# Two-model kernel on one core: a mixer's token-major weight chunks reshaped to 512 outputs, and three stretches of hand-written engine order rewritten

## The chip, the core and the metric

The kernel runs on one core of one Trainium2 chip. The time is the device time of one execution in microseconds; lower is better. The core has a matrix engine (TensorE, called PE in the rows), a vector engine (VectorE, DVE), an activation engine (ScalarE, ACT), a general engine (GpSimd, POOL) and a queue engine (SyncE, SP). DMAs are issued from SP, ACT and POOL.

## What is computed

Two stacked blocks over x of 256 tokens by 1024 features. The first block is one layer of sliding-window attention with sinks and a gated FFN; the second has a two-headed mixer ("ab"), an FFN with squared ReLU, latent attention ("c"), and a second such FFN. In the reference, cut to the part around the change:

```python
def ab_mixer(h, w_in, conv_w, gate_b, head_g, v_g, ws, bs, w_out):
    p = h @ w_in                                   # 1024 -> 3088
    qk, va, oa, gates, uv = jnp.split(p, [2*A_WIDTH, 3*A_WIDTH, 4*A_WIDTH, 4*A_WIDTH + 4*A_HEADS], axis=-1)
    qk = jax.nn.silu(centred_dwconv(qk, conv_w))   # five taps along the tokens
    g = (gates + gate_b)                           # 16 columns: input and forget gates, both ways
    ...
    h_fwd = mlstm_scan(q, k, v, li_f, lf_f)        # and backwards
    ha = rms_norm_2(h_fwd + h_bwd, head_g) * jax.nn.sigmoid(oa)
    u, vb = jnp.split(jax.nn.gelu(uv), 2, axis=-1)
    vb = rms_norm_2(vb, v_g)
    sp = jnp.einsum("gts,bnsgc->bntgc", ws, vb) + bs.T[:, :, None]
    hb = u * sp
    return jnp.concatenate([ha, hb], axis=-1) @ w_out
```

## The kernel before

All weights stream through four slots of 2048 columns each (`SLOTS`, `SLOT`). A chunk of weights is 1 MB: it is loaded by SP into `w_raw`, ACT copies it to `w_hi` in the reduced format that TensorE multiplies (`high`, L682), DVE forms the rest `w_lo = w_raw - w_hi` (`low`, L1209, a "low" in what follows), and TensorE makes three products, hi by hi, lo by hi, hi by lo (`product`, L1921 to L1923). SP may refill a slot when its low is done, ACT may overwrite `w_hi` when the matmuls of the slot's last chunk are done. The two token tiles (128 tokens each) are called t = 0 and 1.

Each engine runs its list in the order in which the code is written; `wait_ge` on a semaphore holds back everything behind it on that engine. `high_upto(n)` and `low_upto(n)` put the conversions of all chunks up to n at that place of the list. So the order in the source is the schedule.

Three stretches matter.

The end of the attention: `out_part(i, t, j)` multiplies chunk i of the output weights for token tile t and half j of the 1024 outputs into bank 4 + 2t + j. When a tile's two halves are complete, DVE adds them to the residual, ACT squares, POOL forms `mean_sq` and `rstd` (L555, L556), DVE normalises (L1229), and TensorE transposes the tile (L1992). `enter` on PE, ACT and DVE carries this into the FFN's first two chunks.

The mixer's input: thirteen chunks `c[0]` to `c[12]`. `c[0]`, `c[1]` (values v) and `c[2]`, `c[3]` (values vb) are token-major: the tokens are the stationary operand and 256 weight columns move (`plain_visit`). `c[4]` is the 16 gate columns, `c[5]` to `c[8]` are q and k, `c[9]`, `c[10]` are u, `c[11]`, `c[12]` the output gate, all feature-major (`projection`). After `c[4]` ACT adds the gate bias (`g_raw`, L935) and sends the rows by four small DMAs to `g4` (L938). DVE then takes minus the absolute value of the forget gates (L1566), ACT the exponential and logarithm (L944, L945), and DVE the running sums and maxima (`gate_rows`, L1573 to L1584). `conv(i)` (L1556) is the convolution of `c[5 + i]`. TensorE needs `g_rows_ready` after `c[8]`. The rest of the mixer follows: `decay_rows` (L2304), `scores_T`, `summed` (L2332), `spatial_mixing` (L2343, needs `vn_ready`, DVE L1617), `outputs_T` (L2373, needs `hn_ready`, DVE L1666).

The mixer's output: `operand_out(o[k], ...)` over four chunks in the order 2, 3, 0, 1 of the operand, whose low parts are `full_low` (L1612), counted by `ab_lo`.

Of the kernel before, what the change touches and what calls it, by code (L numbers as in the profile page):

```python
# [19 lines left out]
F32 = mybir.dt.float32  # L20
# [49 lines left out]
def weight_schedule():  # L70
# [65 lines left out]
def build(nc, t_in, out):  # L136
# [3 lines left out]
    with ctx:  # L140
# [287 lines left out]
        def _(sp):  # L428
# [51 lines left out]
            with sp.Fori(0, N1 - 3) as it:  # L480
# [10 lines left out]
            at = ([i * CW for i in (4, 5)] + [uv + i * CW for i in (2, 3)] + [4 * AW] + [i * CW for i in range(4)]  # L491
                  + [uv + i * CW for i in (0, 1)] + [3 * AW, 3 * AW + CW])
            for a, ch in zip(at, sched["ab_in"]):
                load(ch, cols(w, a, ch.shape[1]))
# [44 lines left out]
        def _(pool):  # L539
# [81 lines left out]

            def masks(h):
# [24 lines left out]
            next_gain(5)  # L647
# [5 lines left out]
            for i, (t, j) in enumerate(LATENTS):  # L653
                pool.wait_ge(S["c_ssq"], i + 1)
                step(pool.tensor_scalar(c_ms[:, t, j:j + 1], c_ss[:, t, j:j + 1], c_ev[:, t:t + 1], 0.0, ALU.add, ALU.add))
                pool.tensor_tensor(c_rs[:, t, j:j + 1], c_ms[:, t, j:j + 1], minus_half[:, 0:1], ALU.pow).then_inc(S["c_rstd"], 1)
            for n in range(QUADS):
# [8 lines left out]
        def _(act):  # L666
# [57 lines left out]
            def enter(use, n, early, then):  # L724

                sum_squares(n, 0)
                transposed_high(use, 0, (0,))
                sum_squares(n, 1, (0,))
                transposed_high(use, 0, (1,))
                sum_squares(n, 1, (1,))  # L730
                high_upto(early)
# [102 lines left out]
            enter(1, 1, 0, c[3].index + 1)  # L834
# [55 lines left out]
            def mixing_values(i):  # L890
                ch = c[i]
                act.wait_ge(S["mm_done"], ch.index + 1)
                for t in range(NT):
                    last = act.activation(ab_v1[:, t, 2 * i:2 * i + 2, 0:AD],
                                          bank[AB_BANK[i]][:, t * 256:t * 256 + 256].rearrange("p (a b) -> p a b", a=2),
                                          ACT.Copy, scale=ab_rc[:, t:t + 1])
                last.then_inc(S["v1_ready"], 1)

            def spatial_values(i):
                ch = c[2 + i]  # L900
                act.wait_ge(S["mm_done"], ch.index + 1)
                for t in range(NT):
                    last = act.activation(ab_vb[:, t, i * CW:(i + 1) * CW], bank[AB_BANK[2 + i]][:, t * CW:(t + 1) * CW],
                                          ACT.Gelu_apprx_tanh, scale=ab_rc[:, t:t + 1])
                last.then_inc(S["vb_ready"], 1)
# [1746 lines left out]
```

## Time and profile before

| | |
|---|---|
| median of three runs | 880.72 us (879.99 to 880.95) |
| the profiled execution | 878.9 us |
| its span, first to last instruction | 877.2 us |
| PE busy | 858.1 us |
| mean granted TensorE clock over the span | 0.994 of full |

The profiled execution is 1.8 us faster than the median, and 1.7 us of its time lie outside the span. A busy PE means that some matmul is in flight; matmuls overlap, so the pace is read from the distance between starts, not from the length of one. An engine's idle time is put down to what ended it. Times in rows are counted from the span's start.

### The profile page before, as it was taken

Reading aid. Unit: us, or ns where it says so; the run is one execution under the profiler, and the core shown is the slowest. Engines: PE = TensorE matmul, PEld = TensorE weight load, DVE = VectorE, ACT = ScalarE, POOL = GpSimd, SP = SyncE. Lnnn points to the kernel's source line nnn. Section 1 sums busy time; section 2 is a strip of 40 time slices with the busy share of each in tenths; the row PEclk is TensorE's granted clock in tenths of the full one; section 3 lists DMA queues with packets and bytes.
Section 4 is the critical chain, followed back from the end, with each engine's and each line's share of the span. In section 5 each row is a group of like instructions: output and inputs, shape, how many; then the busy total and the mean of one; then the engine's idle time right before and its main releaser. Section 6 shows DMA issues by size and latency. Waiting matters only on the chain.

```text
span 877.2 us, 14208 instructions
## 1 busy us (share of the span) xinstructions
PE 858.1 (98%) x5784; PEld 774.5 (88%) x5784; DVE 541.6 (62%) x590; ACT 434.5 (50%) x595; POOL 48.1 (5%) x113
## 2 busy tenths in 40 slices
PE   8999999999999989999999999999999999999996
PEld 8977899999998988889999999999867999999995
DVE  5897554444448669777765555567576675555553
ACT  6675443343344785553744444436465364444431
POOL 2200000000001100310000000003000000000000
PEclk9999999999999998999999999999999999999999
DMA  9644355545555655337575555453602576555601
GB/s 314 226 155 147 121 182 190 193 156 191 188 192 148 221 164 174 115 98 216 177 247 183 184 187 189 135 169 105 230 1 91 195 229 195 181 184 183 190 38 49
DMA packets 98442, 147.68 MB, mean 168 GB/s; under 512 B 4042, under 2 KB 81938, under 8 KB 98402
## 3 DMA queue, kind: packets, MB, share of 16 engines
q1 hardware_dynamic: 97234, 143.11, 50.0%
q0 software_dynamic: 1120, 4.00, 1.6%
q8 instruction: 28, 0.46, 0.2%
q14 instruction: 12, 0.10, 0.0%
q10 hardware_dynamic: 48, 0.02, 0.0%
HBM read 146.05 MB, written 1.05 MB: 168 GB/s over the span
## 4 chain that ended last, share of the span: by engine, by line
PE 92%; DVE 4%; ACT 1%; POOL 1%; issue 1%; DMA 1%; ACTq 0%; DVEq 0%; POOLq 0%
PE bank L1921 28%; PE bank L1922 27%; PE bank L1923 27%; PE bank L1992 1%; PE bank L2579 1%; PE bank L2602 1%; PE bank L2564 1%; PE bank L2558 1%; PE bank L2121 1%; PE bank L2140 1%; DMA x_norm<-arena 1%; DVE w_lo L1209 1%; PE bank L2332 0%; PE bank L2304 0%; PE bank L2044 0%
## 5 line engine op out<-in xcount | busy, mean ns | idle before, releaser
L1209 DVE TENSOR_TENSOR w_lo<-w_raw,w_hi 128x2048 fp32r<-128x2048 f32 (+3 forms) x129 | 289.5, 2252 | 150.9 <-ACT w_hi L682 150.7
L1921 PE MATMUL bank<-xT_hi,w_hi 128*128 128x256 f32 x1068 | 306.0, 286 | 4.3 <-DVE w_lo L1209 4.2
L1923 PE MATMUL bank<-xT_hi,w_lo 128*128 128x256 f32 x1068 | 304.0, 285 | 0.0
L1922 PE MATMUL bank<-xT_lo,w_hi 128*128 128x256 f32 x1068 | 304.0, 285 | 0.0
L682 ACT ACTIVATE w_hi<-w_raw 128x2048 fp32r<-128x2048 f32 (+3 forms) x129 | 241.2, 1877 | 92.4 <-PE bank L1923 85.2
L1921 PEld LDWEIGHTS bank<-xT_hi,w_hi 128*128 128x128 f32 x1068 | 205.6, 192 | 9.3 <-DVE w_lo L1209 4.4
L1922 PEld LDWEIGHTS bank<-xT_lo,w_hi 128*128 128x128 f32 x1068 | 205.7, 193 | 1.9 <-issue 0.2
L1923 PEld LDWEIGHTS bank<-xT_hi,w_lo 128*128 128x128 f32 x1068 | 205.6, 193 | 0.2
L1921 PE MATMUL bank<-w_hi,ff_hi 128*128 128x512 f32 x344 | 134.8, 392 | 0.0
L1922 PE MATMUL bank<-w_lo,ff_hi 128*128 128x512 f32 x344 | 134.5, 391 | 0.0
L1923 PE MATMUL bank<-w_hi,ff_lo 128*128 128x512 f32 x344 | 134.0, 390 | 0.0
L1921 PE MATMUL bank<-w_hi,xT_hi 128*128 128x512 f32 (+3 forms) x216 | 76.0, 352 | 2.3 <-DVE w_lo L1332 1.5
L1923 PEld LDWEIGHTS bank<-w_hi,ff_lo 128*128 128x128 f32 x344 | 64.7, 188 | 13.8
L1921 PEld LDWEIGHTS bank<-w_hi,ff_hi 128*128 128x128 f32 x344 | 64.8, 188 | 12.6 <-issue 0.3
L1922 PEld LDWEIGHTS bank<-w_lo,ff_hi 128*128 128x128 f32 x344 | 64.8, 188 | 11.7
L1923 PE MATMUL bank<-w_hi,xT_lo 128*128 128x512 f32 (+3 forms) x216 | 73.4, 340 | 0.0
L1922 PE MATMUL bank<-w_lo,xT_hi 128*128 128x512 f32 (+3 forms) x216 | 73.3, 339 | 0.0
L1027 ACT ACTIVATE arena<-bank 128x512 f32<-128x512 f32 x30 | 17.8, 595 | 106.4 <-PE bank L1923 106.4
L1702 DVE TENSOR_TENSOR arena<-arena 128x512 f32<-128x512 f32 x30 | 20.7, 691 | 60.2 <-ACT arena L1027 60.2
L1921 PEld LDWEIGHTS bank<-w_hi,xT_hi 128*128 128x128 f32 x216 | 40.8, 189 | 7.7 <-DVE xT_lo L1325 1.6
L1923 PEld LDWEIGHTS bank<-w_hi,xT_lo 128*128 128x128 f32 x216 | 40.8, 189 | 4.2
L1922 PEld LDWEIGHTS bank<-w_lo,xT_hi 128*128 128x128 f32 x216 | 40.9, 189 | 3.7
(269 smaller groups left out, 768.6 us busy)
## 6 DMA issues: line engine op xcount, KB each, us to landing
w_raw<-in_ffn_w SPq DMA_DIRECT2D x64, 1024.0 KB, 5.4
w_raw<-in_ffn_w_gate_up SPq DMA_DIRECT2D x22, 1024.0 KB, 5.1
w_raw<-in_ab_w_in SPq DMA_DIRECT2D x12, 1024.0 KB, 6.1
w_raw<-in_ffn_w_down SPq DMA_DIRECT2D x11, 1024.0 KB, 5.0
w_raw<-in_swa_w_in SPq DMA_DIRECT2D x5, 1024.0 KB, 10.9
w_raw<-in_swa_w_out SPq DMA_DIRECT2D x4, 1024.0 KB, 6.3
w_raw<-in_ab_w_out SPq DMA_DIRECT2D x4, 1024.0 KB, 4.9
w_raw<-in_c_w_out SPq DMA_DIRECT2D x4, 1024.0 KB, 6.6
```

The lines of the kernel that those rows point to most:

```text
L682: act.activation(view(w_hi, ch), view(w_raw, ch), ACT.Copy).then_inc(S["hi_done"], 1)
L1027: act.activation(ff_act[:], bank[buf][:].rearrange("p (a b) -> p a b", a=2), ACT.Relu).then_inc(S["ff2_relu"], 1)
L1209: dve.tensor_tensor(view(w_lo, ch), view(w_raw, ch), view(w_hi, ch).bitcast(F32), ALU.subtract).then_inc(S["lo_done"], 1)
L1702: dve.tensor_tensor(ff_h[:], ff_act[:], ff_act[:], ALU.mult).then_inc(S["ff2_h"], 1)
L1921: pe.matmul(out, sh, mh, start=first, stop=False)
L1922: pe.matmul(out, sh, ml, start=False, stop=False)
L1923: return pe.matmul(out, sl, mh, start=False, stop=last)
L1992: last = pe.transpose(bank[2 * t + half][:, k * P:(k + 1) * P], x_norm[:, t, kk * P:(kk + 1) * P], ident[:])
L2121: last = pe.matmul(bank[e][:, cs], swa_qT[at, n, qs], swa_kT[at, g, ks], start=True, stop=True)
L2140: last = pe.transpose(bank[b][:, i * P:(i + 1) * P], swa_s[:, g % 3, j, 1 + part * P:1 + (part + 1) * P], ident[:])
L2558: pe.matmul(bank[score_bank(p, e)][:, t * SEQ:(t + 1) * SEQ], c_qn[at, p, t * P:(t + 1) * P], c_kn[at, p, :], start=t == 0, stop=False)
L2564: last = pe.matmul(bank[score_bank(p, e)][:, t * SEQ:(t + 1) * SEQ], c_qr[at, p // 2, t * P:(t + 1) * P], c_kr[at, :], start=False, stop=t ...
```

## The change

It does these things.

1. The first four mixer chunks are cut the other way. `c[0]` and `c[1]` are the upper and lower half of the 1024 input features for all 512 outputs of v, `c[2]` and `c[3]` the same for vb. `plain_visit` moves 512 columns into one bank per token tile (4, 5 for v, 6, 7 for vb), and a bank is complete only after the second of the two chunks. ACT reads a whole bank at once (`mixing_values`, `spatial_values`).
2. The four `g4` DMAs are issued by POOL, not ACT.
3. In the mixer DVE's list has the lows of `c[7]` and `c[8]` ahead of its wait for `g4`, `conv(0)` ahead of `gate_rows`, and the later lows between the convolutions in another order. ACT's exponential and logarithm stand behind the reading of `c[5]`.
4. `decay_rows(2)` is ahead of `summed(0)` on TensorE. The first output chunk starts with token tile 1 (`ts=(1,)`) with `ab_lo` at 2, ahead of the wait for `num_ready` 8. On DVE `full_low(4)` and `(5)` are ahead of `normalised_outputs(1)`, and a low is behind it.
5. At the attention's end `swa_values(3)` is one part earlier and `out_part(2, 1, 0)` two parts later, so tile 0 is complete a part earlier. In `enter`, the low of the FFN's second chunk is two halves in two places, and tile 1's transposes stand inside the second visit.
6. POOL's `next_gain(5)`, a DMA for the last norm, is behind the small operations of the latent norm.

```diff
-        add("ab_in", (KT, 16 if i == 4 else CW))
+        add("ab_in", (KT // 2, 2 * CW) if i < 4 else (KT, 16 if i == 4 else CW))
...
+            pool.wait_ge(S["g_raw_ready"], 1)
+            for k in range(4):
+                pool.dma_start(g4[:, k, :], g_raw[4 * k:4 * k + 4, :]).then_inc(S["g4_loaded"], 16)
...
-            def enter(use, n, early, then):
+            def enter(use, n, second, then):
+
+                def part(half):
+                    dve.wait_ge(S["hi_done"], second.index + 1)
+                    k = slice(4 * half, 4 * half + 4)
+                    return dve.tensor_tensor(view(w_lo, second)[:, k], view(w_raw, second)[:, k],
+                                             view(w_hi, second)[:, k].bitcast(F32), ALU.subtract)
 
                 add_residual(n, 0)
-                low_upto(early)
+                part(0)
                 normalise(n, 0, x_norm)
                 add_residual(n, 1, (0,))
-                transposed_low(use, 0, (0,))
+                transposed_low(use, 0)
                 add_residual(n, 1, (1,))
-                transposed_low(use, 0, (1,))
+                part(1).then_inc(S["lo_done"], 1)
+                split[0] += 1
                 normalise(n, 1, x_norm)
...
             transposed_low(2, 1)
             dve.wait_ge(S["params_ready"], 1)
-            low_upto(c[6].index + 1)
+            low_upto(c[8].index + 1)
...
-            low_upto(c[7].index + 1)
+            conv(0)
...
             gate_rows()
-            for i in range(4):
-                conv(i)
-                low_upto(c[min(8 + i, 10)].index + 1)
+            low_upto(c[9].index + 1)
+            conv(1)
+            low_upto(c[10].index + 1)
             dve.wait_ge(S["g_cols_psum"], 1)
             dve.tensor_copy(ab_t.rearrange("p t k h -> p (t k h)"), bank[1][:, 0:32]).then_inc(S["g_cols_ready"], 1)
-            low_upto(c[8].index + 1 + SLOTS)
+            conv(2)
+            conv(3)
+            low_upto(c[11].index + 1)
...
-            low_upto(c[11].index + 1 + SLOTS)
-            normalised_outputs(1)
             full_low(4)
             full_low(5)
+            normalised_outputs(1)
+            low_upto(c[11].index + 1 + SLOTS)
...
+            swa_values(3)
             out_part(2, 0, 0)
-            swa_values(3)
             out_part(2, 0, 1)
-            out_part(2, 1, 0)
             out_part(3, 0, 0)
             out_part(3, 0, 1)
+            out_part(2, 1, 0)
             out_part(2, 1, 1)
             out_part(3, 1, 0)
             out_part(3, 1, 1, norm=1)
...
-                    last = product(bank[AB_BANK[i]][:, t * CW:(t + 1) * CW], uT_hi[:, t, k, :], uT_lo[:, t, k, :],
-                                   hi[:, k, :], lo[:, k, :], k == 0, k == KT - 1)
+                    kt = KT // 2 * half + k
+                    last = product(bank[4 + 2 * (i // 2) + t][:], uT_hi[:, t, kt, :], uT_lo[:, t, kt, :], hi[:, k, :], lo[:, k, :],
+                                   half == 0 and k == 0, half == 1 and k == KT // 2 - 1)
...
-            decay_rows(2)
...
+            pe.wait_ge(S["ab_lo"], 2)
+            pe.wait_ge(S["sig_ready"], 2)
+            operand_out(o[0], AB_OUT_ORDER[0], first=True, ts=(1,), done=None)
+            pe.wait_ge(S["num_ready"], 8)
+            operand_out(o[0], AB_OUT_ORDER[0], first=True, ts=(0,), done=(0, 1))
             pe.wait_ge(S["ab_lo"], 4)
-            pe.wait_ge(S["num_ready"], 8)
-            pe.wait_ge(S["sig_ready"], 2)
-            operand_out(o[0], AB_OUT_ORDER[0], first=True)
```

What this does to DVE's list in the mixer, before. The number behind `w_lo` is the slot; here `w_lo3`, `w_lo1`, `w_lo0` are the lows of `c[5]`, `c[6]` and `c[7]`, and L1573 begins the gate rows.

```order
L1209 TENSOR_TENSOR w_lo3<-w_raw3,w_hi3 128x2048 [waits hi_done,params_ready]
L1209 TENSOR_TENSOR w_lo1<-w_raw1,w_hi1 128x2048 [waits hi_done]
L1566 SCALAR_TENSOR_TENSOR arena<-x_norm 4x512 [waits g4_loaded]
L1209 TENSOR_TENSOR w_lo0<-w_raw0,w_hi0 128x2048 [waits hi_done]
L1573 SCALAR_TENSOR_TENSOR arena<-x_norm,arena 4x512 [waits g_ln_ready]
L1577 SCALAR_TENSOR_TENSOR arena<-one,arena 4x256 [waits dve_chain]
```

And the same place of DVE's list in the change, where L1555 is the convolution:

```order
L1201 TENSOR_TENSOR w_lo3<-w_raw3,w_hi3 128x2048 [waits hi_done,params_ready]
L1201 TENSOR_TENSOR w_lo1<-w_raw1,w_hi1 128x2048 [waits hi_done]
L1201 TENSOR_TENSOR w_lo0<-w_raw0,w_hi0 128x2048 [waits hi_done]
L1201 TENSOR_TENSOR w_lo2<-w_raw2,w_hi2 128x2048 [waits hi_done]
L1565 SCALAR_TENSOR_TENSOR arena<-x_norm 4x512 [waits g4_loaded]
L1555 SCALAR_TENSOR_TENSOR arena<-arena,pcols 128x256 [waits conv_begun,qk_padded]
```

The lows of `c[7]` and `c[8]` (slots 0 and 2) now stand ahead of the wait for `g4_loaded`; before, the low of `c[8]` stood behind the wait, the gate rows and `conv(0)`.

DVE's list where it enters the first FFN, before; `w_lo3` is the FFN's second chunk:

```order
L1255 TENSOR_TENSOR x_res<-x_res,bank 128x512 [waits acc_done] x2
L1209 TENSOR_TENSOR w_lo3<-w_raw3,w_hi3 128x2048 [waits hi_done]
L1229 SCALAR_TENSOR_TENSOR x_norm<-x_res,rstd,gain 128x512 [waits rstd_ready,gain_loaded]
L1229 SCALAR_TENSOR_TENSOR x_norm<-x_res,rstd,gain 128x512
L1255 TENSOR_TENSOR x_res<-x_res,bank 128x512 [waits acc_done]
```

And in the change:

```order
L1247 TENSOR_TENSOR x_res<-x_res,bank 128x512 [waits acc_done] x2
L1255 TENSOR_TENSOR w_lo3<-w_raw3,w_hi3 128x1024 [waits hi_done]
L1221 SCALAR_TENSOR_TENSOR x_norm<-x_res,rstd,gain 128x512 [waits rstd_ready,gain_loaded]
L1221 SCALAR_TENSOR_TENSOR x_norm<-x_res,rstd,gain 128x512
L1247 TENSOR_TENSOR x_res<-x_res,bank 128x512 [waits acc_done]
L1228 TENSOR_TENSOR xT_lo<-bank,xT_hi 128x512 [waits xTh_ready] x2
L1247 TENSOR_TENSOR x_res<-x_res,bank 128x512 [waits mm_done]
L1255 TENSOR_TENSOR w_lo3<-w_raw3,w_hi3 128x1024 [waits hi_done]
```

Only half of the low is left between the residual and tile 0's norm; the other half stands ahead of tile 1's norm.

DVE's list at the mixer's end, before; L1659 is the sum of squares that POOL waits for, L1666 is `normalised_outputs(1)`, L1612 `full_low(4)` and `(5)`:

```order
L1659 TENSOR_REDUCE arena<-arena 128x4 [waits dve_chain]
L1209 TENSOR_TENSOR w_lo0<-w_raw0,w_hi0 128x2048 [waits hi_done]
L1666 TENSOR_TENSOR arena<-arena 128x512 [waits h_rstd]
L1612 TENSOR_TENSOR xT_lo<-arena,xT_hi 128x2x128 [waits ab_hi] x2
L1672 SCALAR_TENSOR_TENSOR arena<-bank,pcols,arena 128x256 [waits hT_psum,sig_ready]
```

And in the change:

```order
L1661 TENSOR_REDUCE arena<-arena 128x4 [waits dve_chain]
L1613 TENSOR_TENSOR xT_lo<-arena,xT_hi 128x2x128 [waits ab_hi] x2
L1668 TENSOR_TENSOR arena<-arena 128x512 [waits h_rstd]
L1201 TENSOR_TENSOR w_lo0<-w_raw0,w_hi0 128x2048 [waits hi_done]
L1674 SCALAR_TENSOR_TENSOR arena<-bank,pcols,arena 128x256 [waits hT_psum,sig_ready]
```

The two `full_low` stand where the low stood, and the low is behind the norm.

## Rows read from the trace of the kernel before

**Rows 1.** The page, busy time of TensorE.

```profile
PE 858.1 (98%) x5784; PEld 774.5 (88%) x5784; DVE 541.6 (62%) x590; ACT 434.5 (50%) x595; POOL 48.1 (5%) x113
```

**Rows 2.** TensorE's waits: engine, line, waited for, total us, times, longest.

```profile
PE bank L1921 <- DVE w_lo L1209: 4.2, 1, 4.2
PE bank L1992 <- DVE x_norm L1229: 2.4, 2, 2.0
...
PE bank L1921 <- DVE xT_lo L1612: 0.7, 1, 0.7
...
PE bank L2373 <- DVE arena L1666: 0.6, 1, 0.6
PE bank L2332 <- DVE arena L1605: 0.4, 1, 0.4
```

**Rows 3.** Stretches: length, PE, PEld, DVE, ACT, POOL busy, PEclk, DMA.

```profile
326.00:330.30 4.30, 0.11 (x1) 0.00 (x0) 4.23 (x7) 4.23 (x5) 0.00 (x0) 1.00 0.00 0
332.00:334.00 2.00, 2.00 (x12) 2.00 (x11) 1.95 (x5) 0.00 (x0) 0.00 (x0) 0.51 1.06 361
334.00:337.00 3.00, 3.00 (x27) 3.00 (x27) 2.96 (x4) 0.00 (x0) 0.00 (x0) 1.00 0.25 87
348.00:350.00 2.00, 2.00 (x11) 2.00 (x11) 2.00 (x2) 1.99 (x7) 0.00 (x0) 0.50 0.49 141
```

**Rows 4.** Timeline of TensorE at 256 columns, first and last of 70 starts.

```profile
254.90 0.28 PE L1921 MATMUL bank<-xT_hi,w_hi 128*128 128x256 f32 x1
...
263.18 0.28 PE L1921 MATMUL bank<-xT_hi,w_hi 128*128 128x256 f32 x1
```

**Rows 5.** Chain that ended last, two 512-column matmuls, six starts apart.

```profile
279.10 0.23 PE bank L1922
...
280.47 0.23 PE bank L1922
```

**Rows 6.** Timeline where tile 0 leaves the attention.

```profile
84.57 2.29 DVE L1209 TENSOR_TENSOR w_lo<-w_raw,w_hi 128x2048 fp32r<-128x2048 f32 x1
85.52 1.51 POOL L555 TENSOR_SCALAR mean_sq<-ssq 128x1 f32<-128x1 f32 x1 [41.27 <-ACT x_norm L714]
87.79 1.41 DVE L1229 SCALAR_TENSOR_TENSOR x_norm<-x_res,rstd,gain 128x512 f32<-128x512 f32 x2 [0.93 <-POOL rstd L556]
...
88.69 1.23 PE L1992 MATMUL bank<-ident,x_norm 128*128 128x128 f32 x8 [2.04 <-DVE x_norm L1229]
```

**Rows 7.** Timeline of ACT's issues and DVE at the gates.

```profile
309.43 2.59 ACTq L938 DMA_DIRECT2D x_norm<-arena  x4
...
316.18 0.68 DVE L1566 SCALAR_TENSOR_TENSOR arena<-x_norm 4x512 f32<-4x512 f32 x1 [5.64 <-DMA x_norm<-arena]
316.79 2.27 DVE L1209 TENSOR_TENSOR w_lo<-w_raw,w_hi 128x2048 fp32r<-128x2048 f32 x1
...
319.50 0.68 DVE L1573 SCALAR_TENSOR_TENSOR arena<-x_norm,arena 4x512 f32<-4x512 f32 x1 [0.44 <-ACT arena L945]
```

**Rows 8.** Timeline from the last convolution to the spatial mixing.

```profile
345.34 1.92 ACT L993 ACTIVATE arena<-arena 128x2048 f32<-128x2048 f32 x1 [3.03 <-DVE arena L1556]
...
353.19 1.68 POOL L633 TENSOR_TENSOR arena<-arena,minus_half 128x8 f32<-128x8 f32 x1
...
355.98 1.21 DVE L1617 TENSOR_TENSOR arena<-arena 128x1024 f32<-128x1024 f32 x1
...
358.70 1.49 PE L2343 MATMUL bank<-wsT,arena 128*128 128x128 f32 x11
```

**Rows 9.** Timeline of the mixer's end, POOL and DVE.

```profile
385.36 2.16 POOL L632 TENSOR_SCALAR arena<-arena 128x4 f32<-128x4 f32 x1 [12.47 <-DVE arena L1659]
...
400.55 0.69 DVE L1276 TENSOR_TENSOR x_norm<-x_res,gain 128x512 f32<-128x512 f32 x1
```

**Rows 10.** DMA issues of POOL: count, KB each, us to landing.

```profile
gain<-in_ffn_norm POOLq DMA_DIRECT2D x2, 512.0 KB, 4.1
...
gain<-in_c_norm POOLq DMA_DIRECT2D x1, 512.0 KB, 6.8
```

More of the change, by code:

```diff
@@ L656, in _ @@
                 pool.tensor_tensor(c_rs[:, t, j:j + 1], c_ms[:, t, j:j + 1], minus_half[:, 0:1], ALU.pow).then_inc(S["c_rstd"], 1)
+            next_gain(5)
             for n in range(QUADS):
@@ L722, in transposed_high, with enter @@
                                    bank[2 * t + half][:], ACT.Copy).then_inc(S["xTh_ready"], 1)
-            def enter(use, n, early, then):
+            def enter(use, n, then):
                 sum_squares(n, 0)
[L727 to L731, printed above, removed]
+                transposed_high(use, 0)
+                sum_squares(n, 1)
                 transposed_high(use, 1)
@@ L935, in _ @@
             act.activation(g_raw, bank[0][0:16, 0:SEQ], ACT.Identity, bias=gate_b[:]).then_inc(S["g_raw_ready"], 1)
-            act.wait_ge(S["g_raw_ready"], 1)
-            for k in range(4):
-                act.dma_start(g4[:, k, :], g_raw[4 * k:4 * k + 4, :]).then_inc(S["g4_loaded"], 16)
             act.wait_ge(S["pads_ready"], 1)
             act.wait_ge(S["params_ready"], 1)
-            high_upto(c[7].index + 1)
-            spatial_values(1)
-            act.wait_ge(S["g_abs_ready"], 1)
-            step(act.activation(g_w, g_w, ACT.Exp))
-            act.activation(g_w, g_w, ACT.Ln, bias=1.0).then_inc(S["g_ln_ready"], 1)
+            high_upto(c[8].index + 1)
             def pairs(i):
@@ L958, in _ @@
                 last.then_inc(S["conv_begun"], 1)
+                if i == 0:
+                    act.wait_ge(S["g_abs_ready"], 1)
+                    step(act.activation(g_w, g_w, ACT.Exp))
+                    act.activation(g_w, g_w, ACT.Ln, bias=1.0).then_inc(S["g_ln_ready"], 1)
                 high_upto(ch.index + 1 + SLOTS)
@@ L1618, in _ @@
             weighted_scores(1)
+            low_upto(c[12].index + 1)
             dve.wait_ge(S["sp_psum"], 1)
@@ L1960, in token_major, with accumulate @@
                         last.then_inc(S["mm_done"], 1)
-            def accumulate(ch, stat_hi, stat_lo, first=False, end=False, ts=(0, 1), js=(0, 1), phase_end=False, norm=None):
+            def accumulate(ch, stat_hi, stat_lo, first=False, end=False, ts=(0, 1), js=(0, 1), phase_end=False, norm=None,
+                           done=(1, 1)):
                 hi, lo = view(w_hi, ch), view(w_lo, ch)
@@ L2226, in gate @@
                 feature_major(ch, bank[0], **more)
-            enter(1, 1, [by_tile(c[0], halves(0)), by_tile(c[1], halves(1))])
+            first, second = by_tile(c[0], halves(0)), by_tile(c[1], halves(1))
+            first(0, low_count=4 + 1)
+            second(0, at=((4, lambda: transpose_tile(1, 1, (0,))), (6, lambda: transpose_tile(1, 1, (1,)))))
+            first(1, low_count=4 + 3)
+            second(1)
             gate(c[2], 1, between=hidden_transposes("ff1_h", 1, "ff1_t"))
@@ L2256, in plain_visit @@
                     arrived(c[i])
+                if low_count:
+                    pe.wait_ge(S["ab_ul"], low_count)
                 hi, lo = view(w_hi, c[i]), view(w_lo, c[i])
-                for k in range(KT):
-                    if low_count and k % 4 == 0:
-                        pe.wait_ge(S["ab_ul"], low_count + k // 4)
+                half = i % 2
+                for k in range(KT // 2):
                     for kk, action in at:
@@ L2355, in _ @@
             scores_T(1)
+            decay_rows(2)
             summed(0)
-            decay_rows(2)
             spatial_mixing()
```

48 lines of the change are left out of this document (20 added, 28 removed).

## The prediction

> **What bounds the kernel now.** I read the page first: TensorE has a matmul in flight for 858.1 of 877.2 us [rows 1], so time can only come out of its waits, its clock, or the number and width of its matmuls. Next its waits, the whole list being 12 us long [rows 2]: one of 4.2 us for a low of DVE, two of 2.4 us together for the norm in front of the first FFN, and three of 0.7, 0.6 and 0.4 us in the mixer. Then the clock by stretches [rows 3]: TensorE stands from 326.0 to 330.3, and in the stretch behind it the granted clock is 0.51, that is 1.2 GHz where 2.4 is full; from 334.0 it is full again. The same half clock is seen once more at 348 to 350, behind the narrow decay rows. Last the pace: at 256 columns 69 starts take 8.28 us, 0.120 each [rows 4]; at 512 columns six starts take 1.37 us, 0.228 each [rows 5].
>
> What the half clock costs: 256 columns at 1.2 GHz are 0.213 us, 0.093 more than the 0.120 above. The low stretch lasts from 330.3 to about 333.9 and holds 17 matmuls, so it costs 17 x 0.093 = 1.6 us. The second, 347.6 to 351.0 with 16 matmuls, costs 1.5 us.
>
> **The change part by part.** *End of the attention.* The two last parts of tile 0 end one part of six 512-column matmuls earlier, 1.36 us. TensorE does the same work in all, so nothing is lost by it. DVE's adding starts 1.36 us earlier; behind it stands half a low, 1.15 us, for 2.29 [rows 6]. POOL's `mean_sq` took 1.51 us beside that low and ended at 87.03, 0.17 us behind the low's end at 86.86 [rows 6]: a small POOL operation waited for DVE's operation. With the half low POOL should end at about 84.6 for 87.0, and the norm start at 85.3 for 87.8. TensorE reaches the transposes at 86.5 as before. The wait of 2.0 us is gone, and of the gap around it (2.2 us in the starts) all. At tile 1 the wait is 0.4 us [rows 2]; its transposes now stand inside the second visit, 2.9 us of matmuls later, so the norm, at about 92 us, is in time. With the pipeline's refill around both I take 0.7 for that: 2.9 us in all. Both ends: 2.2 (only tile 0) and 3.1. The halved low is needed at 91.9 and done at 91.0.
>
> *512 columns.* 192 matmuls of 256 become 96 of 512: 192 x 0.120 - 96 x 0.228 = 1.15 us less. Against it: the second visit is to tile 1's first half, 2.7 us behind the first, where it used to be 2.9 behind; its transposes, ACT's copy and DVE's low part come in between, and I estimate a new wait of 0.25. The low of `c[2]` is about 0.2 late, since ACT's squares in front of its high come a microsecond later. Net 0.7, between 0 (these eat all) and 1.15.
>
> *The 4.2 us wait.* TensorE waits for the low of `c[8]`. DVE had it behind the wait for `g4`, a low, the gate rows and `conv(0)`. Now it is the third low behind `c[5]`'s: ACT's highs of `c[7]` and `c[8]` follow `g_raw`, which ends at about 309; they end at 311 and 313, and the lows at 313.3 and 315.5. TensorE wants `c[8]` at 325.4. The wait is gone (4.2), and with it the half clock behind it (1.6). ACT is freed of 2.6 us of issues [rows 7], without which those highs would be that much later; this cover is not needed for TensorE, only for the next item.
>
> *What is late next.* `spatial_mixing` needs `vn_ready`. Its chain runs through DVE: `g4`, L1566, the gate rows and four convolutions, then ACT's silu and exponentials, POOL's masks and rstd, L1617. Before, DVE started L1566 at 316.18 and ended `conv(3)` at 345.3, when ACT began [rows 8]. Two lows of 2.27 leave that stretch, and the wait of 0.44 for the logarithm [rows 7], for a copy of 0.18 that comes in: 4.8 us less, if `g4` lands at the same time. So `vn_ready` is at 357.2 - 4.8, and 1.1 less because DVE is free and the sum of squares is done when POOL comes: L1617 stood from 355.98 to 357.19 [rows 8], behind POOL's power, which ended at 353.19 + 1.68 = 354.87 [rows 8]; now it starts with it, at 350.1, and ends at 351.3. TensorE would be there at 358.7 [rows 8] - 0.7 - 4.2 - 1.6 - 0.4 = 351.8 with the second half clock, and 350.3 without it. So the second half clock decides little: TensorE either runs slowly or waits. Mixing starts at 351.3 to 351.8 for 358.7; I take 7.1 us. The 0.4 of `summed(0)` [rows 2] is in this, as `decay_rows(2)` (1.05 us) now fills it.
>
> *`g4` through POOL.* The four issues on ACT began at 309.43, 2.59 us long, and DVE went on at 316.18 [rows 7], 4.2 us behind their end. Of POOL's DMAs the trace shows only large ones: 4.1 to 6.8 us from issue to landing, for 512 KB [rows 10]. With issues of 0.6 us the last starts at 311.1 and lands between 315.2 and 317.9 by these. DVE is busy with lows until 315.5 anyway. I take the near end, as 4 KB is nearest to the shortest: no delay, at most 2.3 us later. The Trainium skill, "SBUF — State Buffer", section "SBUF: two separate sides", warns against this very move: a DMA issued from GpSimd has its descriptors written by GpSimd's cores, which some DVE operations lock out, and it advises issuing from ACT. The section "Who interferes with whom" of the same page exempts a two-input subtraction like the low, as an inference. By the first rule `g4` would go out only behind the lows, which is the second size of a rival below; by the exemption nothing changes.
>
> *Mixer's end.* The wait of 0.7 for `full_low` shrinks as two of four are enough, and that of 0.6 for the norm goes: POOL's operation took 2.16 us beside a low, to 387.5 [rows 9], and has no low beside it now. But DVE's own list from there to tile 0's residual is nearly as long as before: four lows of 2.28, and the sums. It starts 7.1 earlier and saves 0.3 on POOL. TensorE's transposes wait for x_norm, whose second half began at 400.55 [rows 9] and would now at 393.2, while TensorE could be there at 392.3: a new wait of about 1 us. I take 0.3.
>
> *The rest.* `next_gain(5)` off POOL's path: its operations for tile 1 start behind ACT's squares, not behind the DMA: 0.
>
> **Sum.** 2.9 + 7.1 + 0.3 = 10.3 us. Against the profiled execution 878.9 - 10.3 = 868.6. That execution is 1.8 us below the median of the three runs, so for the median 880.72 - 10.3 = 870.4.
>
> **The rivals.**
> - *More is gained.* If the second half clock goes too and `g4` lands early, TensorE's path sets the time: 2.9 + 0.7 + 4.2 + 1.6 + 1.5 + 0.4 + 0.7 + 0.6 = 12.6, 868.1. Against it stands the DVE chain to `vn_ready`, which has no slack. 13%.
> - *`g4` is late by POOL.* At 6.8 us to landing 1.7 to 2.3 us less, 872.7. If the lows up to 315.5 hold POOL back, the last transfer lands at 315.5 + 4.1 = 319.6, 3.4 us later than before, 873.8. For: POOL's small operations waited for lows twice [rows 6, 9]. Against: these compute, they are no issues. The lock that the Trainium skill's page on the SBUF describes is this second size. 16%.
> - *A half clock more.* The new waits (0.5 us at mixing, 1 us at the end) stand close behind narrow matmuls; one more stretch at 1.2 GHz costs 1.5 us on TensorE's path, two nearly 3: 871.9 to 873.4. The trace has it behind a stand of 4.3 us, not behind one of 2.2 us (86.5 to 88.7). 12%.
> - *No change.* The wait only moves: `g4` lands 9 to 11 us late, at about 326, and mixing waits for it. 4%.
> - *Slower.* The same mechanism further on: if POOL's four DMAs run one behind the other at 6.8 us each [rows 10], the last lands at 309.3 + 27.2 = 336.5, 20.3 us late, and 20.3 - 10.3 = 10 us is lost: 890.7. It decides from a landing at 326.5. The small transfers' issues would have to be serial; ACT's four took 6.8 us together, from 309.43 to 316.18 [rows 7]. 3%.
> - *As forecast*, 52%.
>
> **How the numbers follow.** The range goes from 867.3 (the larger gain, with something of the 1.8 us between execution and median) to 874.0 (`g4` held back by the lows, or two more stretches at half clock). A measurement of this kernel can tell 0.2%, 1.8 us. Faster by more than that holds in the first three cases and the forecast: 0.93; the same 0.04; slower 0.03.
>
> **What would show it.** In the profile of the changed kernel: no wait on L1209's successor above 0.3 us, no wait on x_norm at 86 us; full clock around `c[8]`; L1565 starting at about 313 (all is 3 us earlier by then) with little idle time in front of it; `mean_sq` of about 0.5 us at tile 0; a wait of TensorE for L1618 or a second stretch at half clock, not both; L1995 waiting about 1 us at the mixer's end. Wrong would be a `g4` that lands past 317 on the old scale, or a DVE idle for over 1 us in front of L1565, and any wait above 2 us at mixing.

## The result, and the profile after

| | before | changed |
|---|---|---|
| median, both on one chip | 880.36 us (878.09 to 880.95, 4 runs) | 866.15 us (865.33 to 867.82, 4 runs) |
| ratio, 95% interval | | 0.9846 [0.9823, 0.9869] |
| the profiled execution, its span | 878.9, 877.2 us | 865.3, 863.6 us |
| mean granted clock of the span | 0.994 | 0.998 |

The change takes 14.2 us off, where 10.3 were forecast; 866.15 lies 1.2 us below the range given. The direction was right, and too little of it was expected. Nine executions of the same changed kernel on two more chips gave 865.3 to 867.4 (medians 866.63 and 865.75, with 878.92 and 878.94 for the kernel before): the gain is 12.3 to 13.2 us there. In the five sets of 9 to 17 executions that were taken beside the experiments the kernel before has its median at 878.92 to 879.68. So 0.7 to 1.4 of the 14.2 us look like luck of the draw: three of the four executions behind 880.36 lie at 880.0 to 881.0, an upper level that is treated further down.

The page of the changed kernel, busy time, and then its list of TensorE's waits, whole, which answers to [rows 1] and [rows 2]:

```profile
PE 852.1 (99%) x5688; PEld 765.2 (89%) x5688; DVE 541.1 (63%) x591; ACT 434.0 (50%) x591; POOL 48.5 (6%) x117
```

```profile
PE bank L1923 <- DVE w_lo L1331: 1.9, 3, 1.5
PE bank L2047 <- DVE arena L1195: 1.1, 1, 1.1
PE bank L1995 <- DVE x_norm L1275: 0.7, 1, 0.7
PE bank L2143 <- DVE xT_lo L1414: 0.7, 1, 0.7
PE bank L2465 <- DVE x_norm L1763: 0.3, 1, 0.3
```

The wait of 4.2 us and the two for the norm are gone, and so are the 0.7, 0.6 and 0.4 us in the mixer; the 1.9 and the 1.1 stand in the program's first part, which the change leaves alone. One wait is new, L1995 for `x_norm` at the mixer's end, as forecast. There are 96 matmuls fewer.

The clock by stretches, where before it was at half in two places [rows 3]; same columns:

```profile
322.00:330.00 8.00, 7.90 (x69) 7.67 (x68) 7.86 (x15) 5.37 (x8) 0.00 (x0) 1.00 0.40 138
334.00:338.00 4.00, 4.00 (x22) 2.75 (x22) 3.96 (x6) 2.38 (x2) 0.00 (x0) 1.00 0.00 1
338.00:342.00 4.00, 4.00 (x35) 3.97 (x34) 2.12 (x2) 3.97 (x11) 1.44 (x6) 1.00 0.76 257
```

Full clock in all. The narrow decay rows stand at 334.0 to 335.9, so the last two stretches hold and follow them.

The timeline of the changed kernel where tile 0 leaves the attention [rows 6 before], then at the gates [rows 7], then from the last convolution to the spatial mixing [rows 8]:

```profile
82.64 1.22 DVE L1255 TENSOR_TENSOR w_lo<-w_raw,w_hi 128x1024 fp32r<-128x1024 f32 x1
83.59 0.44 POOL L556 TENSOR_SCALAR mean_sq<-ssq 128x1 f32<-128x1 f32 x1 [39.92 <-ACT x_norm L719]
84.80 1.42 DVE L1221 SCALAR_TENSOR_TENSOR x_norm<-x_res,rstd,gain 128x512 f32<-128x512 f32 x2 [0.94 <-POOL rstd L557]
...
304.67 6.70 DVE L1201 TENSOR_TENSOR w_lo<-w_raw,w_hi 128x2048 fp32r<-128x2048 f32 x3 [2.16 <-ACT w_hi L687]
305.26 2.06 POOL L625 DMA_DIRECT2D x_norm<-arena  x4 [3.47 <-ACT arena L930]
311.28 0.67 DVE L1565 SCALAR_TENSOR_TENSOR arena<-x_norm 4x512 f32<-4x512 f32 x1
...
335.60 1.92 ACT L985 ACTIVATE arena<-arena 128x2048 f32<-128x2048 f32 x1 [3.77 <-DVE arena L1555]
343.01 1.68 POOL L638 TENSOR_TENSOR arena<-arena,minus_half 128x8 f32<-128x8 f32 x1
344.72 1.23 DVE L1618 TENSOR_TENSOR arena<-arena 128x1024 f32<-128x1024 f32 x1 [0.75 <-POOL arena L638]
346.08 1.20 PE L2352 MATMUL bank<-wsT,arena 128*128 128x128 f32 x9
```

`mean_sq` takes 0.44 us beside half a low. The four small DMAs are issued in 2.06 us while DVE is in its lows, and L1565 starts with no idle time behind the last low. So `g4` is no longer waited for; the last of its four parts had landed at 310.56, 0.7 us before. `vn_ready` comes at 345.95, and TensorE begins the mixing at 346.08, with no wait. The issues on the page of the changed kernel (3.1 us is the middle of the four; the last, which decides, took 3.8):

```profile
x_norm<-arena POOLq DMA_DIRECT2D x4, 4.0 KB, 3.1
```

Where the time came from is read from the starts of the same matmuls. For this the changed kernel's second profiled execution (`after_again` below) is used, since it starts the program like that of before (first matmul of `gain_rows` at 4.83 in both; the first one had 4.50, and by 57 us was 0.58 ahead before any edit).

| first matmul of | before | changed | gain so far | forecast |
|---|---|---|---|---|
| tile 0's transposes, L1992/L1995 | 88.69 | 86.50 | 2.2 | 2.2 |
| first hidden transposes, L2027/L2030 | 107.41 | 104.06 | 3.35 | 2.9 |
| gate columns behind `c[8]`, L2293/L2302 | 337.77 | 327.89 | 9.9 | 9.4 |
| `decay_rows(0)` | 344.48 | 334.59 | 9.9 | 9.4 |
| `scores_T(0)` | 353.84 | 342.35 | 11.5 | |
| `spatial_mixing` | 358.70 | 346.67 | 12.0 | 10.0 |
| last matmul of the program | 869.84 | 857.21 | 12.6 | 10.3 |

### The profile page after: what moved, and what is told of

It reads as the page before. It is cut to its first block, busy times and chain, and to the rows that moved or that the text cites. A ratio compares the mean times of both kernels' runs of the same rounds, so it can differ in the third digit from the quotient of the medians.

```text
span 863.6 us, 14014 instructions
## 1 busy us (share of the span) xinstructions
PE 852.1 (99%) x5688; PEld 765.2 (89%) x5688; DVE 541.1 (63%) x591; ACT 434.0 (50%) x591; POOL 48.5 (6%) x117
## 4 chain that ended last, share of the span: by engine, by line
PE 94%; DVE 4%; ACT 1%; issue 0%; POOL 0%; DVEq 0%; POOLq 0%; ACTq 0%
PE bank L1923 28%; PE bank L1924 28%; PE bank L1925 28%; DVE w_lo L1201 1%; PE bank L1995 1%; PE bank L2590 1%; PE bank L2613 1%; PE bank L2575 1%; PE bank L2569 1%; PE bank L2124 1%; PE bank L2143 1%; PE bank L2341 0%; PE bank L2313 0%; PE bank L2047 0%; PE bank L2160 0%
## 5 line engine op out<-in xcount | busy, mean ns | idle before, releaser
L1201 DVE TENSOR_TENSOR w_lo<-w_raw,w_hi 128x2048 fp32r<-128x2048 f32 (+1 forms) x128 | 287.1, 2251 | 151.3 <-ACT w_hi L687 151.0
```

What stands on the lines that cost most here:

```text
L1201: dve.tensor_tensor(view(w_lo, ch), view(w_raw, ch), view(w_hi, ch).bitcast(F32), ALU.subtract).then_inc(S["lo_done"], 1)
```

## The experiments

Seventeen runs, each with one profile: twelve further kernels, and five repeats of kernels already run. With the first profiles of before and changed this makes nineteen profiles. The part of item 4 at the mixer's end and item 6 have no run of their own; what is said of them comes from the trace of the whole change. "dec to scores" is the time from the first decay row to `scores_T(0)`; at full clock it is 7.76 us, with a stretch at half clock in it 9.3.

**One part of the change alone, on the kernel before.** `entry` has item 5 (`swa_values`, the order of `out_part`, `enter`), `wide` item 1, `gates` items 2 and 3 (the DMAs, the lows, `conv(0)`, ACT's list).

> The kernel before with item 5 alone, the attention's end. By the forecast's sum 2.9 us, bounds 2.2 and 3.1: about 877.5 us. The changed kernel showed 3.4 between the same two matmuls, so that is the other size: 877.0. The rival, that the order of the parts only moves the wait from tile 0 to tile 1, gives 880.4. In the trace the wait for x_norm near 86 us should be gone. As the mixer is untouched but begins 3 us earlier, this is also a look at whether both stretches at half clock come again.

Measured: 874.92 us (874.39 to 875.76), ratio 0.9952 [0.9939, 0.9965], 4.1 us by the medians. The trace has 3.3 of it at the FFN's hidden transposes: tile 0's transposes start at 86.53, the hidden transposes at 104.09. Both stretches at half clock are there again, each as long as before (stand and clock behind it, from the mixer's first transposes to the gate columns 60.1 us for 59.9; dec to scores 9.38).

> The kernel before with item 1 alone, 512 columns in the first four mixer chunks. Forecast 0.7 us less, bounds 0 and 1.15: 879.7 us. Rival: the 4.2 us wait for the low of c[8] is set by DVE's chain from g4, and g4 comes out of the same TensorE list, so that what the wide chunks save reaches the end whole or is eaten by the wait. If the low of c[8] comes no earlier, the time stays at 880.4. The changed kernel showed about 0.5 for it.

Measured: 877.95 us (11 runs), ratio 0.9985 [0.9975, 0.9995], 1.0 us. Between the mixer's first transposes and the gate columns 58.74 us for 59.93: 1.2 us. Here `g4` comes 1.2 us earlier (L1566's start, counted from the transposes, at 37.15 for 38.34), and the end of the stand, which hangs on it, follows; the small waits that the wide chunks bring are hidden by the stand. On top of `gates`, with no stand, it is 53.4 for 53.95, 0.6. The forecast's 0.7 holds. The second stretch at half clock is missing in this profile (dec to scores 7.89), and one is there that before did not have, at 88 to 92 us.

> The kernel before with items 2 and 3 alone: g4 issued by POOL, and the order of ACT and DVE in the mixer. If DVE's chain to vn_ready sets the start of the spatial mixing, as I forecast, it comes 6.2 to 7.4 us earlier: 873.0 to 874.2, and TensorE shows a wait there or the second stretch at half clock. If TensorE's own list sets it (the rival that came nearer), 4.2 for the wait, 1.6 and 1.5 for both stretches at half clock: 7.3 or a little more, 873 or less, and neither wait nor half clock.

Measured: 873.46 us (871.17 to 875.28), ratio 0.9938 [0.9924, 0.9953]; the profiled execution is the one of 871.17. Its trace: 53.95 us to the gate columns for 59.93 (5.98, wait and first half clock being 5.8), dec to scores 7.76, the first gate operation (L1565 of the changed kernel) at 315.46, `vn_ready` at 350.23 and the mixing at 350.94. So the rival holds: TensorE neither waits for `vn_ready` nor runs slowly. But the times lie on three levels, and this was the lowest.

> The kernel before with the gates' items alone, once more. Its six times lay at 871.2 (two), 873.4 (two) and 875 (two), and the profile was of 871.2, with full clock throughout. Theory: the levels are stretches at half clock that come in some executions only, and the median is about 873.5 again; a profile of a higher level shows one behind the decay rows (dec 0 to scores 9.3 us for 7.8) or at another place with narrow matmuls. Rival: the levels have another cause, and a slower profile shows full clock.

Measured: 872.78 us (871.37 to 873.44), ratio 0.992 [0.9905, 0.9936]. This time the profiled execution is of the middle level (872.77). The stretch 88 to 92 us, first of `gates`, then of `gates_again`; behind it the matmul in front of which TensorE waited in the latter:

```profile
88.00:92.00 4.00, 3.48 (x23) 3.07 (x24) 3.15 (x6) 1.80 (x5) 0.00 (x0) 1.00 0.00 0
```

```profile
88.00:92.00 4.00, 3.33 (x12) 3.05 (x13) 2.47 (x4) 1.69 (x4) 0.00 (x0) 0.59 0.02 4
```

```profile
88.67 0.61 PE L1997 MATMUL bank<-ident,x_norm 128*128 128x128 f32 x2 [2.04 <-DVE x_norm L1231]
```

The same kernel, the same wait of 2.04 us, and behind it the clock is at 1.2 GHz in one execution and at 2.4 in the other: the hidden transposes come at 108.85 for 107.25, 1.6 us later, of which 0.15 was there before the wait. So a stretch at half clock behind a short wait is a matter of the single execution.

**Is DVE's chain to `vn_ready` at the edge?** In `vn_late` it is longer:

```diff
             conv(2)
+            dve.wait_ge(S["vb_ready"], 2)
+            vb = ab_vb.rearrange("p t (g c) -> p (t g) c", c=P)
+            for _ in range(2):
+                step(dve.tensor_tensor(ab_sq[:], vb, vb, ALU.mult))
             conv(3)
```

> The changed kernel with two more multiplications of 128x1024 on DVE, 1.22 us each, between conv(2) and conv(3); their result is not used. Theory: in the changed kernel DVE's chain to vn_ready (345.95) and TensorE's list (346.08) meet, so 2.4 us more on DVE is 2.3 us more in the end: 868.4, or 870 if TensorE's stand brings a stretch at half clock. Rival: DVE's chain has slack, and less than 1 us of it is seen: 866.2 to 867.

Measured: 868.62 us (868.23 to 868.92), ratio 0.988 [0.9865, 0.9894]. DVE's last link and TensorE in the timeline of `vn_late`:

```profile
348.34 1.23 DVE L1622 TENSOR_TENSOR arena<-arena 128x1024 f32<-128x1024 f32 x1 [2.05 <-POOL arena L638]
349.62 0.60 PE L2356 MATMUL bank<-wsT,arena 128*128 128x128 f32 x3 [1.67 <-DVE arena L1622]
```

All 2.4 us of it reach the end, so in the changed kernel the two lists meet. `rstd_first` makes the same chain shorter: POOL's power ahead of `masks(1)`. It also has the moved low of `norm_first` (below), which acts only behind the mixing, so its median is to be held against that of `norm_first`, 866.1.

```diff
             masks(0)
-            masks(1)
             group_rstd("vb_sumsq", "vb_rstd")
+            masks(1)
```

> The low moved at the mixer's end and POOL's rstd ahead of masks(1), with the decay rows together. DVE's chain to vn_ready ends 1.2 us earlier, but TensorE's own list ends at the same time as before it did: no change of the lower level, 865.3, median 865.5 to 866.2, with single times up to 867.5 where a stretch at half clock comes. Rival: vn_ready was still the bound by some tenths, and 0.3 us more is gained.

Measured: 866.38 us (864.67 to 866.39), ratio 0.9843 [0.9826, 0.9859]. `vn_ready` comes at 345.51, 1.0 us ahead of the mixing at 346.48; from the mixer's first transposes to the mixing it is 72.2 us as in the changed kernel (72.2). So TensorE's own list is as long as DVE's, and shortening DVE's alone gives nothing.

**The DMAs back on ACT** (item 2 undone in the changed kernel):

> The changed kernel with the four g4 DMAs issued by ACT again. They take 2.6 us on ACT ahead of the highs of c[7] and c[8]. DVE's lows of these then come later: the low of c[7] about 2 us, and L1565 begins 2 to 2.6 us behind 311.3. As DVE's chain to vn_ready has 0.1 us of slack, the end is 2 to 2.5 us later: 868.2 to 868.7. Rival: the issue's place is worth nothing, since ACT is ahead of DVE there: 866.2. A gain of the DMA's own speed would show as an earlier landing than with POOL's (issue to landing 3.1 us there).

Measured: 868.71 us (868.70 to 869.80), ratio 0.9886 [0.9872, 0.9901]. The timeline of `g4_act` at ACT, DVE and TensorE, and the clock by stretches:

```profile
305.64 2.56 ACTq L929 DMA_DIRECT2D x_norm<-arena  x4
310.33 4.49 DVE L1200 TENSOR_TENSOR w_lo<-w_raw,w_hi 128x2048 fp32r<-128x2048 f32 x2 [2.73 <-ACT w_hi L683]
314.74 0.67 DVE L1564 SCALAR_TENSOR_TENSOR arena<-x_norm 4x512 f32<-4x512 f32 x1
349.44 0.82 PE L2351 MATMUL bank<-wsT,arena 128*128 128x128 f32 x5 [1.08 <-DVE arena L1617]
```

```profile
336.00:340.00 4.00, 4.00 (x22) 3.45 (x21) 3.89 (x8) 0.94 (x1) 0.00 (x0) 0.72 0.03 11
340.00:344.00 4.00, 4.00 (x31) 4.00 (x30) 3.58 (x3) 3.97 (x9) 0.18 (x1) 0.86 0.41 101
```

The issues hold back the two highs, DVE stands 2.7 us for them, and L1564 begins 2.9 us later than in the changed kernel (counted from the mixer's first transposes, 40.2 for 37.4). Nearly all of it (2.75) arrives at the mixing, where TensorE waits. This comes close to the forecast's picture: DVE's chain is the bound, and the stretch at half clock behind the decay rows (dec to scores 9.25) costs nothing, because without it TensorE would wait 1.5 us more. Only that wait and stretch are both there, where the forecast had one or the other. What item 2 gains here is the issue time on ACT; the transfer is on the path in neither kernel. It is quicker too, though: from the first issue to the last landing 5.2 to 5.3 us by POOL (305.26 to 310.56 in the changed kernel), 6.75 by ACT before [rows 7].

**The lows behind the gate rows.** `c8_late` brings the stand back:

```diff
-            low_upto(c[8].index + 1)
+            low_upto(c[7].index + 1)
...
             gate_rows()
-            low_upto(c[9].index + 1)
             conv(1)
+            low_upto(c[9].index + 1)
```

> The changed kernel with DVE's low of c[8] and c[9] behind the gate rows and conv(1), all else as changed. By the trace L1565 begins when g4 has landed, about 310; the gate rows end at 319.1, conv(1) at 322.7, the low of c[8] at 325.0, and TensorE wants it at 321.5: it stands 3.5 us. If only the stand costs, 869.6. If a half clock of 1.6 us follows as behind the stand of 4.3 us, 871.2. If the second stretch at half clock behind the decay rows comes back with the first, 872.7: then it hangs on the stand, and not on the decay rows.

Measured: 873.70 us over five executions (872.5 to 874.78), and a sixth of 2153.8, of whose cause nothing is known; ratio 0.9938 [0.9925, 0.9951]. The profile of `c8_late`: DVE at the gates, TensorE's wait, the clock.

```profile
311.87 0.68 DVE L1565 SCALAR_TENSOR_TENSOR arena<-x_norm 4x512 f32<-4x512 f32 x1 [1.16 <-DMA x_norm<-arena]
325.42 6.69 DVE L1201 TENSOR_TENSOR w_lo<-w_raw,w_hi 128x2048 fp32r<-128x2048 f32 x3
```

```profile
PE bank L1923 <- DVE w_lo L1201: 4.6, 1, 4.6
```

```profile
323.00:327.00 4.00, 0.16 (x2) 0.00 (x0) 3.93 (x7) 3.13 (x4) 0.00 (x0) 0.94 0.00 0
327.00:332.00 5.00, 4.24 (x20) 4.25 (x21) 5.00 (x3) 0.00 (x0) 0.00 (x0) 0.50 0.61 194
332.00:336.00 4.00, 4.00 (x30) 4.00 (x29) 0.10 (x1) 0.00 (x0) 0.00 (x0) 0.83 1.04 407
```

Three things are read here. With a low less in front, DVE waits for `g4`, and so its landing is seen: L1565 starts 36.4 us behind the mixer's first transposes, where the changed kernel has 37.4. So in the changed kernel `g4` lands up to 1.0 us before DVE asks for it; its own trace has the last landing 0.7 us before L1565 (0.8 in `after_again`). The stand is 4.6 us, not the 3.5 expected (DVE waited for `g4`, 0.6 for ACT's scaling and 0.2 for the logarithm). And the half clock behind it costs 2.6 us, not 1.6: the low stretch lasts from 326.6 to 333.4, 6.8 us, the last 5.6 of them with TensorE at work. The gate columns come 7.3 us later than in the changed kernel, which is 4.7 and 2.6. Dec to scores is 7.76: the second stretch does not come back with the first.

**The order of the decay rows.** `decay_back` undoes that one line of item 4.

> The changed kernel with decay_rows(2) behind summed(0) again, as before. TensorE then waits for DVE's weighted scores at 343.6 (L1606 begins at 342.83 and took 1.15, so 0.4 to 0.8 us), and decay_rows(2) (1.05 us) stands behind it: the spatial mixing begins 0.4 to 0.8 later, 866.6 to 867.0. Rival: vn_ready is later than both, no change: 866.2. If the second stretch at half clock comes back here, the order of the decay rows was what took it away, and it is 1.5 more.

Measured: 866.63 us (866.17 to 867.96), ratio 0.9863 [0.9849, 0.9878]. From `scores_T(0)` to the mixing 4.86 us for 4.32: 0.54 later, and full clock. `narrow_more` has two more calls in front of `decay_rows(0)`:

```diff
+                if h == 0:
+                    for _ in range(2):
+                        pe.matmul(bank[0][:], sel[:, 0, :], g_nM.rearrange("p d t -> p (d t)"), start=True, stop=True)
```

> The changed kernel with two more matmuls of the decay rows (4 rows by 512 columns) in front of decay_rows(0), which write what it then overwrites. By their length of 1.05 us for two instructions, that is 2.1 us in all: 868.3. If such narrow matmuls bring the stretch at half clock behind them, it is now there in the profile, and the time is 869.8. If only a stand of over 3 us does so, it stays at 868.3 and full clock. One more case: DVE's chain is no longer the bound, so nothing is hidden by it.

Measured: 869.65 us (867.36 to 871.38), ratio 0.9893 [0.9872, 0.9914]. The clock by stretches in `narrow_more`:

```profile
336.00:340.00 4.00, 4.00 (x16) 2.13 (x15) 4.00 (x4) 3.20 (x3) 0.00 (x0) 0.98 0.00 1
340.00:344.00 4.00, 4.00 (x24) 4.00 (x24) 1.29 (x2) 3.98 (x10) 2.18 (x9) 0.60 0.77 261
```

With no stand anywhere near, the half clock follows the narrow matmuls. Dec to scores is 10.98, 3.2 more: about 1.7 for the four matmuls and 1.5 for the clock. (Each of the two calls is two matmuls in the trace.) The single times reach from 867.4 to 871.4; what sets them apart was not seen.

**Once more the same kernels.**

> The kernel before, profiled once more. Theory of the stretches that come and go: the first one, behind the stand of 4.3 us, is there again; the second, at 348 to 351, may be missing, and then decay rows to scores take 7.8 us for 9.4. Rival: both are there, since they belong to the kernel.

Measured: 878.97 us, both stretches are there (PEclk 0.57 at 348 to 352, dec to scores 9.38): the rival holds. For the kernel before the second stretch is no chance of one execution.

> The changed kernel once more, to tell what belongs to it and what to one execution. The stretch at half clock behind the decay rows was in the profiled executions of before, of the kernel with the attention's end alone and of the one with g4 back on ACT, and in none of the other seven; each costs 1.5 us. Theory: it is not set by the order of the list but comes or stays away from one execution to the next, so that the times lie in steps of about 1.5 us (865.3 to 867.8 so far), and the landmarks between such stretches agree to 0.1 us. Rival: the changed kernel never has one in the mixer, its times lie within 0.5 us.

Measured: 866.63 us (865.30, 865.89, 867.37, 867.41), ratio 0.9858 [0.9838, 0.9878]; profile at full clock to the last matmul. The two levels are there, and the profile fell on the lower.

> The changed kernel a third time, as partner of the other two: 866.2 to 866.6, with single times between 865.3 and 867.8.

Measured: 865.75 us (865.31 to 867.08), ratio 0.9847 [0.9831, 0.9864]; full clock again, and the landmarks agree with those of `after_again` to 0.04 us as far as the mixing.

**The new wait at the mixer's end.** In `norm_first` one low stands behind tile 0's norm.

```diff
             low_upto(o[0].index + 1 + SLOTS)
-            low_upto(o[1].index + 1 + SLOTS)
...
                 for j in range(2):
                     add_residual(n, 0, (j,))
                     gained(n, 0, j)
+                if between:
+                    low_upto(between)
```

> The changed kernel with one low of DVE (of the FFN's second chunk) moved from in front of tile 0's last residual to behind its two multiplications by the gain, at the mixer's end. There L1995 waits 0.7 us for x_norm, 1.1 us between its starts. By the trace the residual could begin at 382.9 for 385.0, so the wait goes and 0.7 to 1.1 us with it: 865.1 to 865.4. Rival: the low is then late for the second chunk, or transposed_low behind it is, and the wait only moves: 866.2.

> The kernel with the low moved behind tile 0's gain at the mixer's end, now beside the changed kernel on one chip. Its trace had 1.0 us less between outputs_T(1) and the last matmul (480.3 for 481.3), but a stretch at half clock at 8 to 12 us in the profiled execution. Theory: 1.0 us faster than the changed kernel, 865.2 for 866.2. Rival: the two medians agree within 0.4.

Measured: 866.12 us (864.86 to 866.39), and beside the changed kernel 866.13 for 866.63, ratios to before 0.9851 [0.9838, 0.9863] and 0.9853 [0.9835, 0.9871]. The wait is gone from the list, and from `outputs_T(1)` to the last matmul it is 480.3 us for 481.3. Yet the medians can't tell the two kernels apart: both profiled executions have a stretch of half clock at 8 to 12 us, where the edit changes nothing, which none of the changed kernel's three has. (`vn_late` and `c8_late` have one there as well, so it is no mark of this edit.)

**The decay rows apart.** `decay_split` is `norm_first` with `decay_rows(1)` behind `projection(10)`; `split_rstd` has POOL's swap of `rstd_first` as well. So `rstd_first` and `split_rstd` differ in the split alone.

> The kernel with the low moved at the mixer's end, and decay_rows(1) behind projection(10), so that two calls of the narrow matmuls no longer stand together. Theory: if these bring the stretch at half clock, the times lose their upper level, and the median is 0.5 to 1 below its partner's: 865.2 for 866.1. Rival: the levels come from other places (8 to 12 us, where some profiles had one), and nothing changes; or the later decay_rows(1) makes ACT's exponentials and the weighted scores late, at most 1 us more.

> The decay rows apart and the low moved at the mixer's end, as in decay_split, and POOL's rstd for the mixing ahead of masks(1). By the trace rstd can start at 341.9 for 345.1, vn_ready is at 345 for 348.3, and TensorE comes at 346.9: the stand of 1.5 to 2.1 us is gone, 865.1, and the times lie within 0.5 us of each other. Rival: masks(1) is now late for DVE's weighted scores, which stand behind, and the wait moves to summed(1): 866.8 again.

Measured: `decay_split` 866.81 us (866.63 to 866.90), ratio 0.9857 [0.9839, 0.9875]; `split_rstd` 865.32 us (864.92 to 865.65), ratio 0.9833 [0.9817, 0.9849]. In `decay_split` ACT's second exponentials come later, POOL's mask waits for them with the power behind it, and `vn_ready` is at 348.33 with TensorE there at 346.9. In `split_rstd` that is mended:

```profile
342.76 1.68 POOL L638 TENSOR_TENSOR arena<-arena,minus_half 128x8 f32<-128x8 f32 x1
345.27 1.22 DVE L1620 TENSOR_TENSOR arena<-arena 128x1024 f32<-128x1024 f32 x1
347.45 1.95 PE L2353 MATMUL bank<-wsT,arena 128*128 128x128 f32 x16
```

The nine times of both have no upper level (0.3 and 0.7 us wide), while `rstd_first`, the same without the split, spreads over 1.7 and the changed kernel over up to 2.5. `split_rstd` has the lowest median of all; its interval still overlaps that of the changed kernel.

## Why the forecast was too small, point by point

**Right.** What bounds the kernel, the wait of 4.2 us and the half clock behind it: 6.53 us between hidden transposes and gate columns, where 0.7 + 4.2 + 1.6 = 6.5 were forecast. Tile 0's exit, 2.2. The new wait at the mixer's end, forecast about 1 us, is 0.7 in the list and 1.1 in the starts. No wait of TensorE behind the mixer is new or longer, so nothing shows a cost of item 6. POOL's DMAs were not held back: issued beside two-input subtractions they landed in 3.1 us, the last in 3.8, ahead of need by 0.7. The Trainium skill, "SBUF — State Buffer", section "Who interferes with whom", exempts such an operation as an inference; this case agrees with it.

**Wrong: "So `vn_ready` is at 357.2 - 4.8, and 1.1 less"**, and with it "Mixing starts at 351.3 to 351.8" and "TensorE either runs slowly or waits". On the scale of before `vn_ready` came at 349.9. The chain from L1565 to the end of `conv(3)` fell from 29.1 to 24.3 us, the 4.8 forecast. But the 351.3 leaves L1565 where it was, at 316.18, though the lows were forecast to end at 315.5 and the landing from 315.2 on: it began at 315.2 (311.87 + 3.35), 1.0 earlier, with the landing at 314.4 (311.07 + 3.35). By the forecast's own two numbers 0.7 of this could have been had. From `conv(3)` to `vn_ready` 0.4 more went. These 1.4 us put the chain just ahead of TensorE's 350.0, and the alternative fell away: in this kernel there was neither wait nor half clock. It took both. The shorter chain explains that TensorE did not wait; with a stretch at half clock it would have come at about 351.5 all the same, and why none was there is open (below). `vn_late`, `rstd_first` and `gates` show how close the two lists lie, and `g4_act` shows nearly the forecast's case, with a chain 2.9 us longer. The rival "more is gained" had the mechanism right; "no slack" was argued against it from a number that was 1.4 us off. Even that rival's 868.1 is 2.0 above the measured 866.15, by the step to the median below.

This step is worth 1.5 of the 2.3 us that the trace gained beyond the forecast: 2.1 between gate columns and mixing (1.6 clock, 0.54 decay rows) where 0.6 was left. The rest are sizes. Tile 1's exit was put at 0.7 and is 1.16. The mixer's end was put at 0.3 and is 0.6. Of the 3.9 us by which the medians beat the forecast 1.6 are outside this table, in the next step.

**Wrong: the step from the profiled execution to the median.** The forecast added the 1.8 us between 878.9 and 880.72 to the result, as if both kernels shared them. In the runs of before beside `after_again`, 880.80, 880.84 and 881.06 have a granted clock of 0.990, the other six (878.09 to 879.05) 0.993 to 0.995. So the 880.7 belongs to executions with more time at half clock: by the rounded figures 0.004 of 877 us, about 7 us at half clock, as much as two stretches of 3.4 us. Part of it may stand behind the last matmul, where every profile has some half clock and it costs nothing. The changed kernel's profiled execution is only 0.8 below its median, not 1.8. One place for a stretch more is shown: the wait of 2.0 us in front of tile 0's transposes. Of the five profiled executions with that wait two have half clock behind it (`wide`, `gates_again`), of the fourteen without it none. Item 5 takes this wait away, and by these counts the chance of the stretch as well; `entry` gains 4.1 by the medians and 3.3 in the trace. That the upper level of before comes from this place was not seen, since no profile of before fell there; one stretch there costs 1.5 us, so it is at most a part. The forecast's sentence that half clock stands behind 4.3 us and not behind 2.2 was one execution's word.

**Open.** What decides on the stretch behind the decay rows. It is there in five of the nineteen profiles (before twice, `entry`, `g4_act`, `narrow_more`) and absent in twelve with the same pair of rows. It doesn't need the stand (`narrow_more`, `g4_act`) and doesn't follow it (`wide`, `c8_late`). With more narrow matmuls it was there in the one profile, and taking the pair apart left times without an upper level, which speaks for the pair; nine times are few. Where the changed kernel's executions of 867.4 us lose their 1.5 us no profile shows.

## What to carry to other kernels

When a wait is taken away, follow both lists to the next meeting point, each from the start that your own numbers give it, and name the slack between them in tenths of a microsecond; here 1.4 us decided whether a term of 1.5 could be had at all. A stand costs its length and, in some or all executions, a stretch at half clock behind it, and behind narrow matmuls there can be one too; so removing them can be worth more in the median than one profile shows: look at the single times and their granted clocks for levels before taking a profile as the typical execution. Issue small DMAs from an engine that nothing waits for: here 2.6 us of issues on ACT made the kernel 2.6 us slower (`g4_act`).

## What was not expected of the hardware

- Behind the same wait of 2.04 us the clock was at full in one execution of a kernel and at 0.59 over 4 us in another.
- Stands of nearly equal length, 4.2 to 4.4 us (before, `entry`) and 4.6 (`c8_late`), were followed by about 3.4 and 6.8 us at half clock, 1.6 and 2.6 us of cost. The 3.6 us stand of `wide` was followed by 3.4 us too. All five profiles with a stand of 3.6 us or more have it.
- POOL's issue of four small DMAs took 2.06 us beside DVE's subtractions, ACT's the 2.56 us of `g4_act`.
